# Attention probabilities of MLA heads 0 to 14: the first three query tiles transposed by VectorE blocks and DMA through DRAM, the fourth on TensorE

## The reference, cut to what matters

```
q_nope, q_rope = q[..., :128], rope(q[..., 128:])          # 16 heads
k_nope, v = kv[..., :128], kv[..., 128:]
for s, e in [(0, 16), (16, 144), (144, 272), (272, 400), (400, 528)]:
    sc = (q_nope[s:e] @ k_nope[:e].T + q_rope[s:e] @ k_rope[:e].T) * scale
    p = softmax(where(causal, sc, -big))
    out[s:e] = p @ v[:e]
y = (out * silu(g)) @ w_out
```

## Time and profile before

| what | us |
|---|---|
| median of 3 runs | 2170.64 (2168.44 to 2171.16) |
| the profiled execution: its time | 2170.27 |
| the profiled execution: its span | 2168.5 |
| PE busy in the span | 2141.5 (99%) |
| POOL busy | 1175.3 (54%) |
| DVE busy | 1284.7 (59%) |

### The profile page before, as it was taken

One profiled execution on the slowest core, in us unless ns is written; L12 is line 12 of the kernel. 1 busy time (PEld: TensorE's weight loads), 2 busy tenths in 40 slices (PEclk: granted clock), 3 DMA queues, 4 the chain that ended last, 5 costly groups with the idle time before them and its releaser, 6 DMA issues.

```text
span 2168.5 us, 50089 instructions
## 1 busy us (share of the span) xinstructions
PE 2141.5 (99%) x20795; PEld 1715.8 (79%) x20795; DVE 1284.7 (59%) x2558; ACT 836.7 (39%) x1726; POOL 1175.3 (54%) x829
## 2 busy tenths in 40 slices
PE   8999999999999999999999999999999999999999
PEld 6888887788888767777777777777779788888877
DVE  5465467877850666666666666666652476656621
ACT  4122212333320354555555555555432444444410
POOL 5555566688766264544555544544566453443455
PEclk9999999999999999999999999999999999999999
DMA  4322323333332143333333333333534322222132
GB/s 131 88 78 78 88 88 91 94 97 97 97 110 96 42 126 87 83 82 83 82 92 83 88 87 91 88 90 92 145 79 126 107 78 54 67 56 54 54 129 95
DMA packets 368490, 193.77 MB, mean 89 GB/s; under 512 B 124411, under 2 KB 348793, under 8 KB 367881
## 3 DMA queue, kind: packets, MB, share of 16 engines
q1 hardware_dynamic: 368074, 190.50, 31.8%
q10 hardware_dynamic: 191, 0.07, 0.0%
HBM read 159.18 MB, written 18.52 MB: 82 GB/s over the span
## 4 chain that ended last, share of the span: by engine, by line
PE 93%; DVE 3%; POOL 1%; ACT 1%; issue 1%; DMA 0%; SPq 0%; DVEq 0%; POOLq 0%; ACTq 0%
PE ps L1452 21%; PE ps L161 16%; PE ps L162 15%; PE ps L163 15%; PE ps L1691 4%; PE ps L1707 3%; PE ps L1566 2%; PE ps L1737 2%; PE ps L1680 2%; PE ps L2791 2%; PE ps L1606 1%; PE ps L1651 1%; PE ps L1599 1%; PE ps L1638 1%; PE ps L2775 1%
## 5 line engine op out<-in xcount | busy, mean ns | idle before, releaser
L152 POOL TENSOR_TENSOR w_lo<-raw,w_hi 128x1024 fp32r<-128x1024 f32 (+1 forms) x163 | 416.1, 2553 | 13.6
L149 POOL TENSOR_SCALAR w_hi<-raw 128x1024 fp32r<-128x1024 f32 (+1 forms) x163 | 182.3, 1118 | 399.6 <-PE ps L163 383.2
L161 PE MATMUL ps<-h_hi,w_hi 128*128 128x512 f32 x616 | 242.9, 394 | 2.9 <-DVE h_lo L1129 1.7
L162 PE MATMUL ps<-h_lo,w_hi 128*128 128x512 f32 x616 | 240.8, 391 | 0.0
L163 PE MATMUL ps<-h_hi,w_lo 128*128 128x512 f32 x616 | 240.7, 391 | 0.0
L1452 PE MATMUL ps<-mixed_k,raw 128*64 128x264 f32 x1024 | 146.6, 387 | 0.0
L1452 PE MATMUL ps<-mixed_r,raw 128*64 128x264 f32 x1024 | 144.0, 387 | 0.2 <-ACT ws_b L1771 0.2
L161 PEld LDWEIGHTS ps<-h_hi,w_hi 128*128 128x128 f32 x616 | 116.1, 188 | 28.7 <-DVE h_lo L1129 2.6
L1452 PE MATMUL ps<-mixed_g,raw 128*64 128x264 f32 x1024 | 137.6, 387 | 0.0
L163 PEld LDWEIGHTS ps<-h_hi,w_lo 128*128 128x128 f32 x616 | 116.1, 189 | 24.4
L162 PEld LDWEIGHTS ps<-h_lo,w_hi 128*128 128x128 f32 x616 | 116.2, 189 | 23.1
(11 more groups left out here) (499 smaller groups left out, 5793.4 us busy)
## 6 DMA issues: line engine op xcount, KB each, us to landing
raw<-in_rwkv_w_in_dram SPq DMA_DIRECT2D x64, 512.0 KB, 4.4
raw<-in_w_up_dram SPq DMA_DIRECT2D x44, 512.0 KB, 3.9
raw<-in_w_in_dram SPq DMA_DIRECT2D x41, 512.0 KB, 3.9
raw<-in_w_down_dram SPq DMA_DIRECT2D x22, 512.0 KB, 3.5
raw<-in_mla_w_in_dram SPq DMA_DIRECT2D x22, 512.0 KB, 4.0
sb_kept<-xT SPq DMA_DIRECT2D x16, 528.0 KB, 2.6
xT<-sb_kept SPq DMA_DIRECT2D x16, 528.0 KB, 3.8
raw<-in_mla_w_out_dram SPq DMA_DIRECT2D x16, 512.0 KB, 3.6
```

Of the source, the lines that this page charges most:

```text
L149: nc.gpsimd.tensor_scalar(w_hi[s][:, 0:width], raw[s][:, 0:width], 1.0, 0.0, ALU.mult, ALU.add).then_inc(split_hi, 1)
L152: nc.gpsimd.tensor_tensor(w_lo[s][:, 0:width], raw[s][:, 0:width], w_hi[s][:, 0:width].bitcast(F32), ALU.subtract).then_inc(split_ready, 1)
L161: nc.tensor.matmul(dst, w[0], x[0], start=start, stop=False)
L162: nc.tensor.matmul(dst, w[0], x[1], start=False, stop=False)
```

## The change

For heads 0 to 14, tiles 0, 1 and 2 no longer pass through PE. DVE transposes the 32x32 blocks of a tile in place order into wa_in (an SBUF buffer that is free by then; tile 2 uses the space of tiles 0 and 1), and the spill block apart (`blocked`). SP then writes the blocks to a DRAM buffer p_scr in their transposed places, four DMAs a tile (write_blocks, pieces of 128 bytes), waits until these have landed, and reads the buffer into probT, one DMA a tile and a small one for the spill straight from SBUF (read_turned). SP does this between two of its weight loads, in the order of turned_by_dma. Tile 3 of every head, and all of head 15, go as before. The three semaphores are three that the start of the program has used, each at 16 by then.

The core of the diff:

```diff
+        def write_blocks(sp, h, t):
+            sp.wait_ge(p_blocked, LANDED0 + 3 * h + t + 1)
+            if t == 0:
+                ge(sp, p_here, LANDED0 + 96 * h)
+            for a in range(4):
+                sp.dma_start(p_scr[t].rearrange("(b i) q -> i b q", i=32)[:, :, 32 * a:32 * a + 32],
+                             blocks_of(t)[32 * a:32 * a + 32, :].rearrange("i (b j) -> i b j", j=32)).then_inc(p_written, 16)
+
+        def read_turned(sp, h, t):
+            q = slice(P * t, P * t + P)
+            sp.dma_start(probT[:, 0:t + 1, q], p_scr[t].rearrange("(c p) q -> p c q", p=P)).then_inc(p_here, 16)
+            sp.dma_start(probT[0:N_META, t + 1, P * t + P - 32:P * t + P], spill_of(t)[0:N_META, :]).then_inc(p_here, 16)
+
+        def turned_by_dma(sp, h, loads):
+            written = LANDED0 + 192 * h
+            write_blocks(sp, h, 0)
+            write_blocks(sp, h, 1)
+            next(loads, None)
+            sp.wait_ge(p_written, written + 128)
+            ge(sp, oo_mm, h)
+            read_turned(sp, h, 0)
+            read_turned(sp, h, 1)
+            write_blocks(sp, h, 2)
+            next(loads, None)
+            sp.wait_ge(p_written, written + 192)
+            read_turned(sp, h, 2)
...
         def values(pe, h):
...
-            pe.wait_ge(pt_ev, 4 * h + 4)
+            if h < MH - 1:
+                pe.wait_ge(p_here, LANDED0 + 96 * (h + 1))
+            pe.wait_ge(pt_ev, h + 1 if h < MH - 1 else MH + 3)
...
-            turn(pe, h, 0)
-            turn(pe, h, 1)
+            if h == MH - 1:
+                turn(pe, h, 0)
+                turn(pe, h, 1)
...
-            turn(pe, h, 2)
+            if h == MH - 1:
+                turn(pe, h, 2)
             turn(pe, h, 3)
...
+            def blocked(t):
+                dve.wait_ge(sc_norm, 4 * h + t + 1)
+                if t == 0:
+                    ge(dve, p_here, LANDED0 + 96 * h)
+                elif t == 2:
+                    dve.wait_ge(p_written, LANDED0 + 192 * h + 128)
+                nc.vector.transpose(blocks_of(t), prob_cols(t, 0, P * (t + 1)))
+                slot = T2 * (1 - t % 2) + P * (t + 1)
+                nc.vector.transpose(spill_of(t), prob[96:P, slot:slot + 32]).then_inc(p_blocked, 1)
...
-            turned_out(0)
-            turned_out(1)
+            for t in range(2):
+                turned_out(t) if last else blocked(t)
             maximum(2)
...
             normalise(2)
+            if not last:
+                blocked(2)
...
             maximum(3)
...
-            turned_out(2)
+            if last:
+                turned_out(2)
             turned_out(3)
```

More of the change, by code:

```diff
@@ L290, in program @@
         x_copied = sem("x_copied")
-        x_land = [sem(f"x_land{t}") for t in range(QB)]
+        x_land = [sem(n) for n in ("x_land0_p_blocked", "x_land1_p_written", "x_land2_p_here", "x_land3")]
         low = region(0)
@@ L2435, in program @@
         prob = xT[:, 5:7, :].rearrange("p a b -> p (a b)")
+        p_scr = [nc.dram_tensor(f"p_scr{t}", [P * (t + 1), P], F32, kind="Internal").ap() for t in range(QB - 1)]
+        p_blocked, p_written, p_here = x_land[0:3]
+        LANDED0 = 16
         put = region(64)
@@ L2758, in prob_cols, with blocks_of, spill_of, unit_loads @@
             return prob[:, slot + at:slot + at + n]
+        def blocks_of(t):
+            return (wa_in[:, 0:P], wa_in[:, P:3 * P], wa_in[:, 0:3 * P])[t]
+        def spill_of(t):
+            return wa_in[96:P, 3 * P + 32 * t:3 * P + 32 * t + 32]
+        def write_blocks(sp, h, t):
[22 more added lines that the diff above has]
+            read_turned(sp, h, 2)
+        def unit_loads(sp):
+            for unit in MLA_UNITS:
+                load_mla(sp, unit)
+                yield
+            for k in range(3):
+                load_out_rows(sp, k)
+                yield
         def turn_bank(t):
@@ L2763, in spill_cols @@
         def spill_cols(h, t):
-            at = P * min(t + 1, QB - 1)
-            return (turn_bank(t) if t < QB - 1 else value_bank(0) if h < MH - 1 else 2), at
+            return 2 + (t % 2 if t < QB - 1 else 0), P * min(t + 1, QB - 1)
         def turn(pe, h, t):
             pe.wait_ge(sc_norm, 4 * h + t + 1)
-            if h or t >= 2:
-                pe.wait_ge(pt_ev, 4 * h + (0, 0, 1, 2 if h < MH - 1 else 3)[t])
-            if h and t == QB - 1:
+            if t == 2:
+                pe.wait_ge(pt_ev, MH)
+            if t == QB - 1 and h == MH - 1:
+                pe.wait_ge(pt_ev, MH + 2)
                 pe.wait_ge(zt_ev, h)
@@ L2890, in head_act @@
                 act.wait_ge(sc_max, 4 * h + t + 1)
-                if h or t >= 2:
-                    act.wait_ge(pt_mm, 4 * h + max(t - 1, 0))
+                if t >= 2 and h == MH - 1:
+                    act.wait_ge(pt_mm, h + t - 1)
+                elif t >= 2:
+                    act.wait_ge(p_blocked, LANDED0 + 3 * h + t - 1)
+                elif h:
+                    act.wait_ge(p_blocked, LANDED0 + 3 * h)
+                    act.wait_ge(pt_mm, h)
                 dst = prob_cols(t, 0, keys(t))
@@ L2946, in turned_out @@
             def turned_out(t):
-                dve.wait_ge(pt_mm, 4 * h + t + 1)
-                if h:
-                    dve.wait_ge(oo_mm, h)
+                dve.wait_ge(pt_mm, h + 1 + (t if h == MH - 1 else 0))
+                dve.wait_ge(oo_mm, h)
                 bank, at = spill_cols(h, t)
@@ L2953, in turned_out @@
                                       ps[:, turn_bank(t), 0:P * (t + 1)].rearrange("p (a b) -> p a b", b=P)).then_inc(pt_ev, 1)
-            turns = h % 2 == 1 and h < MH - 1
+            def blocked(t):
[7 more added lines that the diff above has]
+                nc.vector.transpose(spill_of(t), prob[96:P, slot:slot + 32]).then_inc(p_blocked, 1)
+            last = h == MH - 1
+            turns = h % 2 == 1 and not last
             maximum(0)
@@ L3012, in _ @@
                     load_in(sp, n)
[L3013 to L3017, removed]
+                loads = unit_loads(sp)
+                for _ in itertools.islice(loads, 6):
+                    pass
+                for h in range(MH - 1):
+                    turned_by_dma(sp, h, loads)
+                for _ in loads:
+                    pass
                 sp.wait_ge(unit_done, UNIT_AT["gate", MH - 1] + 1)
```

## The result

| | before | after |
|---|---|---|
| time, median of 4 runs each on one chip | 2169.54 us (2168.42 to 2171.16) | 2251.6 us (2250.18 to 2253.54) |
| span of the profiled execution | 2168.5 us | 2250.1 us |
| PE busy | 2141.5 us (99%) | 2155.4 us (96%) |

The change makes the kernel slower: after over before is 1.0378 (95% interval 1.036 to 1.0396), 82 us. The forecast was 2255. Its sum is right to 3.4 us, but its two terms are off by 12 and by 10 us in opposite directions: that the sum comes so near is luck, and the terms are what this part is about.

What follows compares the result with a forecast made beforehand. The prediction took PE, busy 2141.5 of 2168.5 us, to bound the kernel, other engines close behind. It added 54 us at fill kb and 30.5 us at values to 2170.3 us, giving 2255 us, range 2215 to 2310.

Steps and rivals of the forecast that it cites:

- First wait: DVE's transpose of tile 2 waits for writes of tiles 0 and 1, so PE waits at fill kb: 54 us.
- I take 0.71: SP's eight writes of tiles 0 and 1 are issued 0.71 us apart.
- I take 2.4: A write of tiles 0 and 1 into DRAM lands 2.4 us after its issue; ends 2.0 and 5.3.
- The low end of the range: At DVE's wait for the writes: 0.55 us an issue and 2.0 us to land, sum 31 us.
- the clock: PE's granted clock, now 0.9 or more: if gaps lower it, PE's matmuls lengthen and the time passes the range.
- The sign that the prediction set for a wrong first term: Writes of tiles 0 and 1 landing before 9 us after the start of values.
- Second wait: PE waits at values for the read of tile 2, issued by SP behind the load of X: 30.5 us.
- the spill, issued about 0.6 later and tiny, lands by then: Tile 2's spill lands by the time PE's values can start after the read of tile 2; no added time.
- Rival 3: Writes in 128-byte pieces into DRAM land in 5.3 us; wait behind them 98 us, total 2299 us; chance 0.17.
- Rival 2: Only the wait for writes shows, none at values for the read of tile 2: 2224 us; chance 0.15.
- Rival 4: Everything at its low end and part of the 14.9 us of transposes comes back: within 0.2%; chance 0.02.
- Rival 1: DVE's wait for writes and PE's for the read both covered, PE loses 135 transposes: 2155 us; chance 0.04.

Runs made afterwards that it cites:

- e1: The changed kernel with SP's read of tile 2 issued ahead of the load of X instead of behind it: 2208.93 us, ratio 1.0175 to the kernel before.
- e2: The changed kernel with tile 2's blocks in a buffer of their own, so DVE needn't wait for the writes of tiles 0 and 1: 2226.61 us, ratio 1.0268.
- e3: The changed kernel with both edits: own buffer for tile 2's blocks, and its read ahead of X's load: 2179.81 us, ratio 1.0047.
- e4: The changed kernel with unused matmuls on PE, eight ahead of the wait at values and six ahead of fill kb: 2247.18 us, ratio 1.0356.
- e7: The kernel before with all the new DMAs beside it, on buffers no engine reads and with no compute engine waiting: 2170.11 us, ratio 1.0004.
- e5: e3 with tile 2's block transpose behind the first kn_lo copy in odd heads, and head 14 turned on PE too: 2168.41 us, ratio 0.9997.
- e9: e5 with POOL splitting X in two parts, PE's rope and v fills waiting for the first alone: 2161.31 us, ratio 0.9959.
- e8: e1 with six unused 128-column matmuls on PE ahead of fill kb: 2199.82 us, ratio 1.0143 to the kernel before.

## Why the prediction was right, and which of its terms were not

- **What bounds the kernel** and both places of waiting: right. e1 and e2 take each away alone, and e3 both, for 71.8 of the 82 us.
- **First wait, forecast 54, measured 41.9.** The step that failed is the issue interval, "I take 0.71", and after it the landing, "I take 2.4". They were 0.46 and 1.7 us: the write that ends last began near V + 7.5 instead of V + 9.05, and the mask of tile 3 came at V + 10.13 instead of V + 12.05. At full clock V to K was 13.5 us, 2.0 more than before in odd heads and 1.5 in even ones, for a forecast of 3.97 and 3.28. The low end of the range (0.55, 2.0 us, sum 31) was nearer to that: 7 x 2.05 + 7 x 1.5 + 2.25 = 27 us. The row of 0.71 was taken because its pieces are alike. It is a mean: the issues in it begin 0.65 us apart, but for one that took 1.57. Why they are 0.65 and not 0.47 apart was not tried.
- **What made up for half of that is a term that the sum left out, the clock, and some late writes.** The prediction named the clock only as a way past its range; it fell, and the time stayed well inside. In the seven heads whose values ran below the full clock, V to K was 107.1 us, 12.6 more than 7 x 13.5. About 10 of these are the clock: DVE begins tile 0's blocks at V + 4.8 to V + 5.4 in them and at V + 3.7 in the other seven, and in e4, where values is at full clock, in all. The other 3 come from three heads in which one of the eight issues took 1.4 us instead of 0.45. One more head, at 14.92, had full clock; its eighth write landed 3.25 us after its issue. Why single issues and landings are that late is open. The sign that the prediction set for a wrong first term, writes that land before V + 9, didn't show either: at full clock they landed at V + 9.2.
- **Second wait, forecast 30.5, measured 40.2** with head 14. The chain was right: POOL's end, SP's X load, then the read, and e1 removes it by order alone. Wrong was the step "the spill, issued about 0.6 later and tiny, lands by then". The spill is issued 0.51 us behind the read and needs 2.8 us in the median, not much less than the read for being 2 KB, so it ends last. In the 13 heads with an X load K to V was 11.33 us in the mean, T + 10.5 instead of T + 10.05, 0.5 us more a head. Four of the 13 are above the others: in two the spill was issued 1.2 and 1.9 us behind the read, in two kb itself ran at the lower clock. Head 13 took 1.55 us for 0.6. Head 14 was put at nothing, "it holds nothing"; there the writes and reads of tile 2 alone cost 2.1 us.
- **The fit of the Trainium skill.** The page "DMA: Bandwidth & Descriptors" of the Trainium skill, section "Anatomy of one DMA", gives 2.0 us plus the bytes, for DMAs issued on another path than SP's. The writes landed below its fixed part (medians of 1.5, 1.7 and 1.8 us for 16, 32 and 48 KB), and the 2 KB spill well above it (2.8). Here the measurement decides. The prediction's total by it, 2242, would have been 9.6 us low.
- **Rival 3, small writes into DRAM are slow:** false. The 5.3 us of that one DMA of 1024 pieces doesn't carry over; writes of 128 to 384 pieces land in 1.5 to 1.8 us in the median, and e7 shows that they hold nothing up.
- **Rival 2, only the writes' wait:** false; its price of 2224 is not what a kernel without the second wait takes either (e1: 2208.9).
- **Rival 4, within 0.2%:** false for this change; e5, with both waits taken away, is what such a result needs.
- **Rival 1, both waits covered, at 2155:** it didn't happen, and its price was wrong too. The prediction credited 14.9 us in full although it had read that DVE and POOL were only 0.2 us ahead of PE at kb and at X. e3 (2179.8) and e5 (2168.4) have both waits covered and gain nothing; e9 shows the engine that took PE's place between K and V.

## What to carry to other kernels

Work taken off the busiest engine is worth only the distance to the next one on the same stretch: read that distance per stretch before pricing a removal, and expect to move the second engine in the same edit. When a step goes out through a queue, count its issues and what stands ahead of it there; the place of one read behind the X load on SP cost 43 us here, nearly twice the DMA traffic (e7) nothing. A new idle stretch of 2 to 3 us on PE is dearer than it looks, since the matmuls behind it may run at the lower clock; in half of the heads here they did. It belongs in the sum, not among the provisos.

## What the runs showed of the hardware that was not expected

- DMA issues from SP differ by kind: 0.46 us for writes into DRAM of 128 or 256 pieces of 128 bytes, 0.54 for 384, and 0.65 for the 256-piece ones within SBUF of the RWKV stage. Single ones take 1.4 to 1.8 us in any of these.
- A transfer of 2 KB within SBUF, issued behind a read of 64 to 192 KB, landed in 2.8 us in the median (1.7 to 3.6), later than 48 KB of small pieces into DRAM (1.8 us).
- Idle stretches of 2.3 to 3.4 us were in half of the heads followed by matmuls at 0.51 of the full clock, and useless matmuls in the gap made a kernel 7 to 9 us faster (e8 against e1).
- 41% instead of 22% of the DMA engines' time cost the kernel nothing (e7).
